# One fp32 transformer pair on a single core: where hB and the split weights lie in on-chip memory

## The reference

```python
# first block
mod = silu(c) @ w_ada + b_ada                  # shift, scale, gate
h = rms(x, norm_g) * (1 + scale) + shift
proj = h @ w_in                                # 2048 x 8192
att = chunk_attention(...) * silu(a_z)         # 8 heads of 128
hg = hgrn2(...) * silu(g_z)                    # 8 gated linear-recurrence heads
x = x + gate * (concat(att, hg) @ w_out)       # 2048 x 2048
# second block
z = rms_norm(x, g_mix_2) @ w_in_2              # 2048 x 1856
mkv = rms_norm(mem_2, g_mem_2) @ w_mem_kv_2    # 2048 x 1024
y = concat(pool_mixer, mla_mixer, memory_cross_attention)
x = x + y @ w_o_2                              # 2048 x 2048
g = rms_norm(x, g_ffn_2) @ w_gate_2            # 2048 x 5632
x = x + (silu(conv(g)) * (rms_norm(x, g_ffn_2) @ w_up_2)) @ w_down_2
```

## Time and profile before

| what | value |
|---|---|
| time, median of 3 runs | 1639.62 us (1639.46 to 1643.21) |
| time of the profiled execution | 1638.8 us |
| its span in the trace | 1637.0 us |
| mean granted TensorE clock | 0.992 |
| PE busy | 1593.5 us, 97% |
| PEld busy | 1409.5 us, 86% |
| DVE busy | 1151.3 us, 70% |
| ACT busy | 860.6 us, 53% |
| mean DMA rate | 202 GB/s |

### The profile page before, as it was taken

The page is one execution under the profiler, slowest core; times in us unless marked ns, Lnnn a source line. Parts: engine busy times, 40 slices in busy tenths (PEclk is TensorE's granted clock), DMA queues, the critical chain, the costliest instruction groups (busy, mean ns, idle before and its releaser), DMA issues.

```text
span 1637.0 us, 24289 instructions
## 1 busy us (share of the span) xinstructions
PE 1593.5 (97%) x9650; PEld 1409.5 (86%) x9650; DVE 1151.3 (70%) x1696; ACT 860.6 (53%) x1321; POOL 137.5 (8%) x164
## 2 busy tenths in 40 slices
PE   8999999988999999898999999999999999999999
PEld 6787789988999999886789888888888888888887
DVE  5888768877677976656677777777777777454544
ACT  6766446667665555454556554444444444444442
POOL 0000000312120320031414000000000000000000
PEclk9999999999999999999999999999999999999999
DMA  9999975513556864432334455554554555555552
GB/s 376 360 360 371 353 264 207 206 65 130 192 186 250 319 226 155 149 135 78 104 129 155 180 180 185 201 198 175 193 206 177 184 206 182 202 182 184 195 187 103
DMA packets 47825, 331.02 MB, mean 202 GB/s; under 512 B 5281, under 2 KB 6689, under 8 KB 8417
## 3 DMA queue, kind: packets, MB, share of 16 engines
q1 hardware_dynamic: 45184, 312.20, 52.1%
q0 software_dynamic: 2240, 17.04, 2.7%
q10 hardware_dynamic: 290, 0.25, 0.1%
HBM read 327.37 MB, written 2.10 MB: 201 GB/s over the span
## 4 chain that ended last, share of the span: by engine, by line
PE 77%; DVE 12%; ACT 5%; issue 3%; DMA 1%; POOL 1%; ACTq 0%; DVEq 0%; POOLq 0%
PE ps L1141 19%; PE ps L1142 10%; PE ps L1137 7%; PE ps L1139 7%; PE ps L1138 7%; PE ps L1196 5%; PE ps L1195 5%; PE ps L1194 5%; DVE wl L1885 4%; DVE raw L1931 3%; ACT wh L1487 2%; DMA raw<-in_wts 1%; PE ps L1319 1%; PE ps L1277 1%; PE ps L1184 1%
## 5 line engine op out<-in xcount | busy, mean ns | idle before, releaser
L1885 DVE TENSOR_TENSOR wl<-raw,wh 128x1024 fp32r<-128x1024 f32 x512 | 624.0, 1232 | 357.3 <-ACT wh L1487 356.7
L1487 ACT ACTIVATE wh<-raw 128x1024 fp32r<-128x1024 f32 x512 | 531.0, 1054 | 372.5 <-PE ps L1196 137.2
L1141 PE MATMUL ps<-hA,wh 128*128 128x512 f32 x1408 | 488.7, 390 | 0.0
L1142 PE MATMUL ps<-hA,wl 128*128 128x256 f32 x1408 | 397.0, 282 | 0.0
L1141 PEld LDWEIGHTS ps<-hA,wh 128*128 128x128 f32 x1408 | 264.4, 188 | 55.3
L1142 PEld LDWEIGHTS ps<-hA,wl 128*128 128x128 f32 x1408 | 266.1, 189 | 0.0
L1137 PE MATMUL ps<-hA,wh 128*128 128x256 f32 x752 | 220.5, 293 | 0.0
L1139 PE MATMUL ps<-hA,wl 128*128 128x256 f32 x752 | 212.6, 283 | 0.0
L1138 PE MATMUL ps<-hA,wh 128*128 128x256 f32 x752 | 212.5, 283 | 0.0
L1137 PE MATMUL ps<-hB,wh 128*128 128x256 f32 x576 | 167.2, 290 | 4.3 <-issue 2.4
L1139 PE MATMUL ps<-hB,wl 128*128 128x256 f32 x576 | 163.7, 284 | 0.0
(11 more groups left out here) (287 smaller groups left out, 2067.5 us busy)
## 6 DMA issues: line engine op xcount, KB each, us to landing
raw<-in_wts SPq DMA_DIRECT2D x256, 1024.0 KB, 4.8
raw<-in_ada SPq DMA_DIRECT2D x36, 1024.0 KB, 5.1
side<-in_ada POOLq DMA_DIRECT2D x12, 1024.0 KB, 7.5
work<-in_memN SPq DMA_DIRECT2D x2, 1024.0 KB, 8.7
xs<-in_xN POOLq DMA_DIRECT2D x1, 2048.0 KB, 18.0
xs<-in_xT POOLq DMA_DIRECT2D x2, 1024.0 KB, 6.4
out_rows<-xs SPq DMA_DIRECT2D x8, 256.0 KB, 2.5
wp<-in_dt SPq DMA_DIRECT2D x8, 128.0 KB, 2.5
```

The lines of the kernel that those rows point to most:

```text
L1141: e.matmul(ps[bank][:, :], w1, hl, start=first, stop=False)
L1142: i = e.matmul(ps[bank][:, T:2 * T], w2, hl[:, 0:T], start=False, stop=last)
L1487: e.activation(wh[:, h % WS, :], raw[:, n % RAW, part * HALF:(part + 1) * HALF], ACT.Copy).then_inc(s_hi)
L1885: e.tensor_tensor(wl[:, h % WS, :], src, wh[:, h % WS, :].bitcast(F32), ALU.subtract).then_inc(s_lo)
```

## The change

`hB` is moved to a multiple of 128 bytes (by padding, and by moving `vs` and `ones` in front of it). `wh` and `wl` become one buffer, `w_ring`, with high and low of a slot side by side. A second name for it, `m_ring`, begins 32 bytes later; halves whose weights will move (`turns(h)`: the kinds `m`, which are memory_row and chunk, and `w_down_2`) are split into `m_ring` and read from it as `mh` and `ml`; the eight blocks of `m` still use `wh` and `wl`. Since a slot of `m_ring` reaches 32 bytes into the next slot of `w_ring`, a half that turns, whose next slot holds a half that doesn't, waits for one half more. From the built program this is so for halves 424, 425 and 426, the first three of down; no other wait has another value. Every engine's instructions are the same in number, kind and order.

Start addresses modulo 128 afterwards: `raw`, `w_ring`, `hA`, `hB` 0; `m_ring`, `hA2`, `hB2`, `xs`, `vs`, `ones`, `early`, `cs`, `cols`, `work` 32. By stage:

| stage | matmuls | stationary, before | moving, before | stationary, after | moving, after |
|---|---|---|---|---|---|
| memory_row, 512 columns | 192 | 64 | 0 | 0 | 32 |
| chunk, 512 | 768 | 0 | 0 | 0 | 32 |
| s over hA, 256 | 1536 | 0 | 0 | 0 | 0 |
| s over hB2, 256 | 1728 | 0 | 96 | 0 | 32 |
| s over hA2, 256 | 720 | 0 | 32 | 0 | 32 |
| gate and up over hA2, 512 and 256 | 2816 | 0 | 32 | 0 | 32 |
| down, 512 | 1056 | 64 | 0 | 0 | 32 |

```diff
@@ -837,24 +837,30 @@
             return t
 
         raw = sb("raw", [P, RAW, 2048])
-        wh = sb("wh", [P, WS, HALF], F32R)
-        wl = sb("wl", [P, WS, HALF], F32R)
+        w_off = at[0]
+        w_ring = sb("w_ring", [P, WS, 2, HALF], F32R)
+        at[0] += 32
+        vs = sb("vs", [P, NVEC])
+        at[0] += (P - at[0]) % (2 * P)
         side = nc.alloc_sbuf_tensor_at("side", [P, 4, D], F32, offset=at[0])
         hA_off = at[0]
         hA = sb("hA", [P, KT, 512], F32R)
-        at[0] += 64
+        at[0] += 32
         xs = sb("xs", [P, KT, T])
+        ones = sb("ones", [P, P])
+        at[0] += -at[0] % P
         early = nc.alloc_sbuf_tensor_at("early", [P, 4096], F32, offset=at[0] + 32)
         E1 = nc.alloc_sbuf_tensor_at("E1", [P, 512], F32, offset=at[0] + 32 + 15 * 2048)[:, :]
         hB_off = at[0]
         hB = sb("hB", [P, KT, 512], F32R)
-        at[0] += 64
+        at[0] += 32
         cs = sb("cs", [P, NCST])
-        vs = sb("vs", [P, NVEC])
         mk = sb("mk", [P, len(LEVELS), P], U8, 1)
         wp = sb("wp", [P, 4, P])
-        ones = sb("ones", [P, P])
         cols = sb("cols", [P, 224])
+        m_ring = nc.alloc_sbuf_tensor_at("m_ring", [P, WS, 2, HALF], F32R, offset=w_off + 32)
+        wh, wl = (w_ring[:, :, i, :] for i in range(2))
+        mh, ml = (m_ring[:, :, i, :] for i in range(2))
         hA2 = nc.alloc_sbuf_tensor_at("hA2", [P, KT, 512], F32R, offset=hA_off + 32)
         hB2 = nc.alloc_sbuf_tensor_at("hB2", [P, KT, 512], F32R, offset=hB_off + 32)
         NW = min((nc.sbuf_top - 64 - at[0]) // 4, 13700)
@@ -947,7 +953,7 @@
         a1 = free_hi = cb_at + D
         AT, a1 = carve(a1, 4, T)
         a1 -= P
-        dl, a1 = carve(a1, 8)
+        dl = cols[:, 152:160]
         free_top = a1
         kn_sq, _ = carve(free_top, 512)
         kn_ss, kn_t, kn_r = (cols[:, 64 + 8 * i:72 + 8 * i] for i in range(3))
@@ -1068,6 +1074,15 @@
                 return after(tile, "act", "ev")
             return after(tile, "dve", "rm" if tile[0] in RMS_TILES else "add")
 
+        entry_of = {b[1]: b[2] for b in o.beats if b[0] == "split"}
+
+        def turns(h):
+            kind, name, _ = o.entries[entry_of[h]]
+            return kind == "m" or name == "w_down_2"
+
+        def weights(h):
+            return (mh, ml) if turns(h) else (wh, wl)
+
         def normed(name):
             return moving["2" if name == "wo" else "3"]
 
@@ -1169,7 +1184,7 @@
                     e.wait_ge(*moving_ready("A", kt))
                 for i in (1, 0) if g == 0 and kt == kts[0] and pair == 0 else (0, 1):
                     c = 2 * pair + i
-                    w1, w2 = wh[:, h % WS, i * 512:(i + 1) * 512], wl[:, h % WS, i * 512:(i + 1) * 512]
+                    w1, w2 = mh[:, h % WS, i * 512:(i + 1) * 512], ml[:, h % WS, i * 512:(i + 1) * 512]
                     if kt == kts[0]:
                         if g == 0 and c in (1, 2):
                             e.wait_ge(*after(("open",), "act", ("xc", 7)))
@@ -1187,7 +1202,7 @@
                 m.then_inc(s_half)
 
             def down_part(h, kt, c, t, first, last):
-                w1, w2 = (w[:, h % WS, c % 2 * 512:c % 2 * 512 + 512] for w in (wh, wl))
+                w1, w2 = (w[:, h % WS, c % 2 * 512:c % 2 * 512 + 512] for w in (mh, ml))
                 hi = hB[:, kt % KT, t * P:(t + 1) * P]
                 lo = hB[:, kt % KT, T + t * P:T + (t + 1) * P]
                 po = ps[DOWN_BANKS[c][t]][:, :]
@@ -1483,8 +1498,8 @@
             def split(h, n, part):
                 e.wait_ge(raw_in[n % RAW], 16 * (n // RAW + 1))
                 if h >= WS:
-                    e.wait_ge(s_half, h - WS + 1)
-                e.activation(wh[:, h % WS, :], raw[:, n % RAW, part * HALF:(part + 1) * HALF], ACT.Copy).then_inc(s_hi)
+                    e.wait_ge(s_half, h - WS + 2 if turns(h) and not turns(h - WS + 1) else h - WS + 1)
+                e.activation(weights(h)[0][:, h % WS, :], raw[:, n % RAW, part * HALF:(part + 1) * HALF], ACT.Copy).then_inc(s_hi)
 
             def rstd(t, dst, t1, t2, pre=""):
                 e.wait_ge(*after(t, "dve", pre + "r1"))
@@ -1882,7 +1897,7 @@
             def split(h, n, part):
                 src = raw[:, n % RAW, part * HALF:(part + 1) * HALF]
                 e.wait_ge(s_hi, h + 1)
-                e.tensor_tensor(wl[:, h % WS, :], src, wh[:, h % WS, :].bitcast(F32), ALU.subtract).then_inc(s_lo)
+                e.tensor_tensor(weights(h)[1][:, h % WS, :], src, weights(h)[0][:, h % WS, :].bitcast(F32), ALU.subtract).then_inc(s_lo)
 
             def rstd_head(t, t1, ss, n, pre="", pe="ss"):
                 e.wait_ge(*after(t, "pe", pe))
```

## The result

The changed kernel took 1643.32 us (median of 20 runs, 1639.65 to 1646.47), the kernel before 1639.55 us in the same session (20 runs, 1635.88 to 1644.64). The ratio is 1.002, with a 95% interval of 1.0011 to 1.003: slightly slower, and the interval leaves out 1. The forecast was 1625.0 with a range of 1619.5 to 1633.5, so it was wrong. The profiled execution took 1640.83 us.

A forecast was written before the change was run, and what follows sets the result against it. PE, busy for 97% of the span, was taken as the bound: matmuls times pitch. Gains of 7.0, 0.5, 4.9 and 2.4 us less 0.8 made 14.0 us off 1638.8; forecast 1625.0 us, range 1619.5 to 1633.5.

The forecast's parts named there:

- hB stationary at 0 and not 64: Down and memory_row: pitch 6.6 ns less per matmul, 7.0 us gained in down and 0.5 in memory_row.
- Rival 2: Down or w_out: the stage, not the address, sets the pitch; 1632.3 us, or 1639.6 without any address effect; chance 0.12.
- The moving weights at 32 and not 0: Down, chunk and memory_row: 1.6 ns less per matmul, together 2.4 us gained; bounds 4.9 gained and 6.4 lost.
- Rival 1: 512-column matmuls: moving weights at 32 cost 3.3 ns each, giving 1633.6 us; chance of a cost above 1 ns 0.20.
- hB2 moving at 32 and not 96: w_out and the mixers' stage: pitch 120.0 to 116.7 ns, gaining 2.5 and 2.4 us, together 4.9.
- The handover: Start of down: three splits wait one half more, so PE's first matmul of half 425 comes 0.8 us late.
- The sum: Whole kernel: 7.0 + 0.5 + 4.9 + 2.4 - 0.8 = 14.0 us off 1638.8, so 1624.8; forecast 1625.0.
- The rule of independent ports: Skill's rule that TensorE's two read ports are independent: pitch the same whatever the address, leaving only the handover in the sum.

The follow-up runs named there:

- e1: Changed kernel with the moving weights back at 0 and without the longer wait, hB still moved; 1637.78 us, ratio 0.9991 to the kernel before.
- e3: Changed kernel with hA itself at 32, hA2 being the same place; 1634.59 us.
- e5: On top of e1, hA and hB both placed at 128 modulo 256, as the weights are; 1630.09 us, ratio 0.9946 to the kernel before.
- e6: On top of e5's places, distance 0 where weights move and 32 where they are stationary, w_in included; 1626.75 us, ratio 0.9928.
- e9: Kernel before with hB and all behind it 192 bytes up, dl put into cols for room; 1630.27 us, ratio 0.9949.
- e2: Changed kernel with hB at 64 again and hB2 at 96, moving weights kept at 32; 1643.05 us.
- e4: Changed kernel with the moving weights 64 bytes behind and not 32; 1635.98 us.
- e11: Changed kernel with the moving weights 96 bytes behind and not 32; 1639.36 us.
- e10: Kernel before with hB and all behind it 64 bytes up, the first part of the change alone; 1636.17 us.
- e12: e5 with the longer wait put back for halves 424 to 426 and nothing else; 1630.66 us.
- e7: On top of e5, gate and up's moving operand at distance 0 (in hA) and not 32; 1629.98 us.

## Why the prediction was wrong

**hB stationary at 0 and not 64: failed.** The step said that "after the change down's stationary operand has the remainder that chunk's has" and that this is worth 6.6 ns. The remainder was taken modulo 128, and of one operand by itself. The trace of before allowed it, since it had only two pairs at 512 columns, one at distance 0 and one at 192. The runs put in its place the distance of the two operands modulo 256, of which I now have all eight multiples of 32, three of them (0, 192 and 224) from more than one pair of addresses modulo 256:

| distance (moving less stationary, modulo 256) | pitch at 512 columns, ns | seen in |
|---|---|---|
| 0 | 226.7 | chunk of before, e1 and e3; both stages of e5; down of e6 and e9 |
| 32 | 233.3 | chunk of the changed kernel and e2 |
| 64 | 228.9 | chunk of e4 |
| 96 | 233.4 | chunk of e11 |
| 128 | 232.4 | down of e1 and e10 |
| 160 | 234.3 | down of the changed kernel and e3 |
| 192 | 233.3 | down of before and of e4 |
| 224 | 233.3 to 233.4 | down of e2 and e11 |

hB at a multiple of 128 moved down from distance 192 to 128 by itself: 0.9 ns (e10), 1.0 us of the 7.0 forecast. To reach 226.7 it had to go to 128 modulo 256 (e9). Rival 2 also left down at 233.3, and its time without any address effect, 1639.6, is the nearest to the 1640.8 of the profiled execution. That is luck: in it the address was not the cause, and e1, e5, e9 and e10 show that it is. I had its period wrong.

**The moving weights at 32 and not 0: failed in sign.** I took 1.6 ns of gain between 3.3 gained and 3.3 lost. In chunk it was 6.6 ns lost, outside both bounds (e1 against the changed kernel); in down 1.9 lost, 232.4 to 234.3. Rival 1 had the sign and half the size. I had the warning in the earlier trace rows and went by the earlier trace rows, where 256 columns gained at the same distance. In chunk 6.6 x 768 = 5.1 us were lost in pitch. Against the kernel before they don't show in the stage, 179.2 both times: 768 matmuls at 226.7 ns are 174.1 us, so 5.1 us of it went beyond the pitch, nearly all in waits, and 768 at 233.3 ns are 179.2. The slower pitch took just the time that PE had spent waiting. Against e1 they show as 3.4 us.

**hB2 moving at 32 and not 96: right in sign, too large.** The pitch went to 117.3 and, in other unbroken rows, 118.7, not 116.7. The distance is 160 there and not hA2's 32, for the same reason as above; e9, with the distance 32, has 116.7. The two stages gave 1.0 and 2.6 us, together 3.6 of 4.9. What is missing is in w_out, 1.0 of 2.5, which I took to have nothing that could hold PE up: 768 x 2.7 ns are 2.1 us, but the largest gap between two starts of its long row grew from 0.42 to 0.92 us, a wait for DVE's split, and three more grew by about 0.1 each.

**The handover: right.** 0.8 us forecast, 0.79 read in the changed kernel and 0.9 by the wait alone (e12), at the matmul and for the tile that the working named.

**The sum.** Down should have become 8.7 us shorter but for the handover's 0.8; it became 1.9 longer (1056 x 1.0 ns and 0.8). Chunk gave nothing of 0.6. The start came 1.1 us late instead of 0.6 early, with a granted clock of 0.97 in memory_row, w_in took 0.6 more, the two hB2 stages gave 3.6, and gate and up lost 1.9, mostly to the clock behind PE's wait for POOL, of which nothing was forecast. 1.9 + 1.1 + 0.6 + 1.9 - 3.6 = 1.9 against a span 2.0 us longer. The start and the clock vary between executions: chunk began between 68.6 and 71.1 us in these profiles, and at 71.1 only here and in e6, the two with a stretch at the lower clock level at 47 us. What can be laid to the change by its stages is down with the handover, 1.9 lost, chunk, nothing, and the hB2 stages, 3.6 gained: 1.7 us faster, where the medians of 20 runs are 3.8 us slower. So the mechanism explains why the forecast gain didn't come, and not the sign of the 0.2%. The mean granted clock of the 20 runs is 0.9885, and that of 45 executions of the kernel before in the sessions of the experiments 0.9914. What the difference can cost is, by an estimate from these, up to 0.0029 of 1640 us, 4.8 us. Whether the layout has a part in the lower clock stays open. The sum itself has a slip that changes nothing: 1624.8 with the 0.8 that it names is 1625.6, not 1625.0.

**The rule of independent ports.** The Trainium skill's page SBUF, State Buffer (Who interferes with whom) would have had no address in the sum. By the earlier trace rows this trace disagreed already. The rule would have given a better time than mine here, for a reason that e1, e5, e9 and e10 contradict: only places changed in e9, and down's pitch fell by 6.6 ns.

**What stays open.** Why the distance counts, and why 64 costs only 2.2 ns at 512 columns in chunk while it costs 7.2 ns for a pair in gate and up, no run shows. Whether the alternation of widths or the stationary role of the weights makes that difference wasn't tried. Distances of 32, 64, 96, 128 and 160 were seen at one pair of addresses modulo 256 each. Those of 32, 64 and 96 were seen in chunk alone and those of 128 to 224 in down alone; only 0 was seen in both, with the same pitch, so that the stage plays no part beside the distance is shown for 0 alone. That 512 is not the period is shown for the distance 0 alone.

## What to carry to other kernels

When two streams of like matmuls have different pitches, write down the start address of both operands modulo 256 and more, and fit the distance between them, not the remainder of one. Two points in a trace can't tell a period of 128 from one of 256; one run that moves a single buffer by 64 or 128 bytes can, and costs two lines. A place that is good for one width and one role (32 behind, 256 columns moving) is not to be carried to another width without a row for it.

## What the runs showed of the hardware

- The pitch of a float32r matmul of 512 columns, in an unbroken row of equal ones at a granted clock of 1.00, went with the distance of the two operands' starts modulo 256 bytes: 226.7 ns at 0, and 228.9 to 234.3 at the seven other multiples of 32, 3% from end to end.
- At 256 columns with stationary weights it was 120.0 ns at distances 0 and 96, 116.7 or 117.8 at 32, and 117.3 or 118.7 at 160. So one and the same distance gives either of two pitches there, in different unbroken rows of one kernel (the changed kernel's w_out and mixers' stage) and in the same row of two kernels with these operands at the same addresses (w_out's 117.3 in the changed kernel and 118.7 in e1). What picks one of the two isn't shown.
- At the start of gate and up the granted clock was 0.50 for some 3 us behind a wait of PE of 1.8 us (e2) and of 2.16 us (the changed kernel), and 1.00 behind waits of 1.8 us (before), 2.5 us (e4) and 2.6 us (e7).
